# Attention outputs times w_out as three products of high and low parts, with w_out loaded raw and split on the chip

## What is computed

```python
for l in range(DEPTH):                                   # 2
    ret_o = retention(rq, rk, r_v, r_g, ret_gn_w[l])      # 256 columns
    swa_o = sliding_window_sink_attention(...)            # 384 columns
    mla_o = latent_attention(...)                         # 384 columns
    mix = jnp.concatenate([ret_o, swa_o, mla_o], axis=-1) @ w_out[l]   # 256x1024 @ 1024x1024
    x = layer_norm(DEEPNORM_ALPHA * x + mix, ln1_g[l], ln1_b[l])
    ffn = grouped_moe(x, router_w, router_bias, exp_w_gate_up[l], exp_w_down[l])
    x = layer_norm(DEEPNORM_ALPHA * x + ffn, ln2_g[l], ln2_b[l])
```

## Time and profile before

| | us |
|---|---|
| median of 3 runs | 1013.22 (1012.91 to 1014.51) |
| the profiled execution, own time | 1014.55 |
| span of its trace, first to last instruction | 1012.8 |
| TensorE busy in the span | 980.8 (97%) |
| VectorE, ScalarE, GpSimd busy | 538.0, 454.1, 92.1 |
| mean granted TensorE clock | 0.993 of full speed |

### The profile page before, as it was taken

One profiled execution on the slowest core, in us unless ns is written; L12 is line 12 of the kernel. 1 busy time (PEld: TensorE's weight loads), 2 busy tenths in 40 slices (PEclk: granted clock), 3 DMA queues, 4 the chain that ended last, 5 costly groups with the idle time before them and its releaser, 6 DMA issues.

```text
span 1012.8 us, 14203 instructions
## 1 busy us (share of the span) xinstructions
PE 980.8 (97%) x5816; PEld 809.3 (80%) x5816; DVE 538.0 (53%) x720; ACT 454.1 (45%) x643; POOL 92.1 (9%) x75
## 2 busy tenths in 40 slices
PE   8999999999999999999999999999999999999998
PEld 8997649777778789975697776787999568999997
DVE  2105637543499361264573336995568536456544
ACT  3354314522387345333452226774477434343331
POOL 0380000000000033540000000000013000000000
PEclk9999998999999999999999999999999999999999
DMA  9910403767799557031167668984223625544531
GB/s 275 292 54 1 166 1 142 284 271 295 287 361 395 135 163 201 1 105 74 42 243 273 271 253 324 375 338 167 84 83 126 218 73 199 211 170 166 202 129 42
DMA packets 88824, 189.75 MB, mean 187 GB/s; under 512 B 24864, under 2 KB 55728, under 8 KB 80448
## 3 DMA queue, kind: packets, MB, share of 16 engines
q1 hardware_dynamic: 86976, 184.23, 50.1%
q0 software_dynamic: 1504, 2.73, 1.1%
q10 hardware_dynamic: 288, 1.99, 0.5%
HBM read 187.90 MB, written 1.05 MB: 187 GB/s over the span
## 4 chain that ended last, share of the span: by engine, by line
PE 85%; ACT 5%; DVE 4%; SPq 3%; DMA 1%; issue 1%; POOL 1%; DVEq 0%; ACTq 0%
PE bank L1172 72%; PE bank L1540 2%; DVE BL L1952 2%; PE bank L1213 2%; PE bank L1570 1%; DMA WE<-in_w_in 1%; SPq L601 1%; ACT BH L855 1%; POOL QL L704 1%; PE bank L1261 1%; PE bank L1554 1%; PE bank L1243 1%; SPq L585 1%; PE bank L1247 1%; PE bank L1271 1%
## 5 line engine op out<-in xcount | busy, mean ns | idle before, releaser
L1952 DVE TENSOR_TENSOR BL<-WE,BH 128x2048 fp32r<-128x2048 f32 x72 | 163.4, 2288 | 26.0 <-ACT BH L855 25.5
L855 ACT CAST BH<-WE 128x2048 fp32r<-128x2048 f32 x72 | 136.4, 1909 | 24.5 <-PE bank L1172 24.5
L1172 PE MATMUL bank<-BH,XSB 128*128 128x512 f32 x256 | 82.3, 391 | 3.3 <-DVE BL L1952 3.3
L1172 PE MATMUL bank<-BH,XSA 128*128 128x512 f32 x256 | 81.9, 391 | 2.8 <-DVE BL L1952 2.8
L704 POOL TENSOR_TENSOR QL<-WE,QH 128x2048 fp32r<-128x2048 f32 (+2 forms) x12 | 49.3, 4126 | 345.2 <-ACT QH L847 345.2
L1172 PE MATMUL bank<-WB,XT 128*128 128x512 f32 x160 | 70.4, 596 | 3.2 <-ACT XT L922 1.3
L1172 PE MATMUL bank<-XTH,WH 128*128 128x256 f32 x256 | 72.6, 284 | 0.8 <-DVE XTL L2111 0.8
L1172 PE MATMUL bank<-XTH,WL 128*128 128x256 f32 x256 | 72.4, 283 | 0.0
L1172 PE MATMUL bank<-XTL,WH 128*128 128x256 f32 x256 | 72.4, 283 | 0.0
L969 ACT ACTIVATE XT<-bank 128x256 f32<-128x256 f32 (+1 forms) x40 | 14.5, 363 | 120.0 <-PE bank L1172 120.0
L2049 DVE SCALAR_TENSOR_TENSOR XT<-XT,small,bank 128x256 f32<-128x256 f32 (+1 forms) x40 | 18.1, 451 | 91.2 <-ACT XT L969 91.1
(11 more groups left out here) (355 smaller groups left out, 2406.8 us busy)
## 6 DMA issues: line engine op xcount, KB each, us to landing
WE<-in_exp_w_gate_up SPq DMA_DIRECT2D x64, 1024.0 KB, 9.1
WE<-in_exp_w_down SPq DMA_DIRECT2D x32, 1024.0 KB, 9.1
WE<-in_w_up SPq DMA_DIRECT2D x16, 1024.0 KB, 5.2
WE<-in_w_down SPq DMA_DIRECT2D x16, 1024.0 KB, 5.6
WE<-in_w_in SPq DMA_DIRECT2D x7, 2048.0 KB, 8.5
WE<-in_w_in SPq DMA_DIRECT2D x8, 1024.0 KB, 8.8
WB<-in_w_out SPq DMA_DIRECT2D x2, 2560.0 KB, 9.6
WE<-in_w_in SPq DMA_DIRECT2D x12, 256.0 KB, 7.3
```

The costliest lines, as they stand in the source:

```text
L855: nc.scalar.copy(BH[pair_of(b)][:, :], raw[b % N_RAW]).then_inc(blk_high[pair_of(b)], 1)
L1172: ins = nc.tensor.matmul(dst, lhsT, rhs, start=first and n == 0, stop=last and n == len(pairs) - 1)
L1952: v.tensor_tensor(BL[pair_of(b)][:, :], raw[b % N_RAW], BH[pair_of(b)][:, :].bitcast(F32), ALU.subtract).then_inc(blk_low[pair_of(b)], 1)
```

## The change

`w_out` of the first block's layers is loaded raw into the expert area `WE` in four DMAs of 1 MB, as soon as the raw projection units are used up. ScalarE casts it into `WB` (high parts) in four pieces of 128x2048, three of them ahead of its sliding-window copies and the fourth after the retention norm. GpSimd subtracts in place in `WE` (low parts). ScalarE's copies of the head outputs become casts into the high part, and VectorE subtracts them from the PSUM bank to get the low part (into `WE` behind `w_out`), which also hands the bank back: TensorE waits for VectorE now where it waited for ScalarE. Each product of `mix_part` becomes three. The second block's `w_out_2` stays as it is.

```diff
+OUT_ORDER = (1, 2, 0, 3)
...
+        out_raw = WE[:, 0:KD * D]
+        OUT_H, OUT_L = over("OUT_H", "WB", 0, [P, KD, D]), over("OUT_L", "WE", 0, [P, KD, D])
+        ATT_H, ATT_L = over("ATT_H", "XT", 0, [P, KD, SEQ]), over("ATT_L", "WE", KD * D, [P, KD, SEQ])
...
@@ SyncE
-                sp.wait_ge(ret_roped, (l + 1) * 2)
-                sp.wait_ge(*full("mla_v1", l))
-                sp.dma_start(w_out[:, 0:C_MLA, :], wo[:, 0:C_MLA, :]).then_inc(wout_in, 16)
-                sp.dma_start(w_out[:, C_MLA:KD, :], wo[:, C_MLA:KD, :]).then_inc(wout2_in, 16)
+                for u in (7, 8, 9):
+                    sp.wait_ge(unit_low[u % 3], projected(l, u))
+                for c in OUT_ORDER:
+                    sp.dma_start(out_raw.rearrange("p (c n) -> p c n", c=KD)[:, 2 * c:2 * c + 2, :], wo[:, 2 * c:2 * c + 2, :]
+                                 ).then_inc(wout_in, 16)
@@ GpSimd, behind the retention gate
+                for n, c in enumerate(OUT_ORDER):
+                    pool.wait_ge(out_high, l * 4 + n + 1)
+                    part = slice(2 * c, 2 * c + 2)
+                    nc.gpsimd.tensor_tensor(OUT_L[:, part, :], out_raw.rearrange("p (c n) -> p c n", c=KD)[:, part, :],
+                                            OUT_H[:, part, :].bitcast(F32), ALU.subtract).then_inc(out_low, 1)
@@ ScalarE, behind the copies of mla_v
+                act.wait_ge(ret_roped, (l + 1) * 2)
+                act.wait_ge(wout_in, (l + 1) * 4 * 16)
+
+                def high_out(c):
+                    part = slice(2 * c, 2 * c + 2)
+                    nc.scalar.copy(OUT_H[:, part, :], out_raw.rearrange("p (c n) -> p c n", c=KD)[:, part, :]).then_inc(out_high, 1)
+
+                for c in OUT_ORDER[:3]:
+                    high_out(c)
...
-                nc.scalar.copy(XT[:, 2:4, :], bank("swa_o0")[:, :]).then_inc(*took("swa_o0"))
+                nc.scalar.copy(ATT_H[:, 2:4, :], bank("swa_o0")[:, :]).then_inc(att_high, 1)
...
                 nc.scalar.activation(grs, grs, ACT.Exp, scale=-0.5).then_inc(gn_rooted, 1)
+                high_out(OUT_ORDER[3])
...
@@ TensorE
-                    return product(bank(f"mix{n}")[:, :], [(XT[:, k, token(n // 2)], w_out[:, k, cols]) for k in chunks], first, last)
-
-                pe.wait_ge(wout_in, (l + 1) * 16)
+                    return product(bank(f"mix{n}")[:, :], [pair for k in chunks for pair in (
+                        (ATT_H[:, k, token(n // 2)], OUT_H[:, k, cols]), (ATT_H[:, k, token(n // 2)], OUT_L[:, k, cols]),
+                        (ATT_L[:, k, token(n // 2)], OUT_H[:, k, cols]))], first, last)
+
+                pe.wait_ge(out_low, l * 4 + 2)
...
+                pe.wait_ge(out_low, l * 4 + 3)
...
-                pe.wait_ge(wout2_in, (l + 1) * 16)
+                pe.wait_ge(out_low, l * 4 + 4)
@@ VectorE, behind the maxima of latent attention
+                def low_heads(n, job, part):
+                    w = (part.stop - part.start) * SEQ
+                    dve.wait_ge(att_high, l * 5 + n)
+                    v.tensor_tensor(ATT_L[:, part, :], bank(job)[:, 0:w].rearrange("p (a b) -> p a b", b=SEQ),
+                                    ATT_H[:, part, :].bitcast(F32), ALU.subtract).then_inc(*took(job))
+
+                low_heads(1, "swa_o0", slice(2, 4))
+                low_heads(2, "swa_o1", slice(4, 5))
...
                                 ).then_inc(ret_out, 1)
+                low_heads(3, "ret_oT", slice(0, 2))
                 softmax_norm("mla", l, link, mla_p1, mla_p0)
...
+                low_heads(4, "mla_o0", slice(5, 7))
+                low_heads(5, "mla_o1", slice(7, 8))
                 for g in range(N_GRP):
```

More of the change, by code:

```diff
@@ L493, in build @@
             "rows_high", "rows_low", "gsel_ready", "sel_made", "gates_ready", "order_ready"))
+        out_high, out_low, att_high = sem("out_high"), sem("out_low"), sem("att_high")
         gathered, silu_done, hid_high, y_high = (sem(n) for n in ("gathered", "silu_done", "hid_high", "y_high"))
@@ L910, in _ @@
                 act.wait_ge(*full("swa_o0", l))
-                nc.scalar.copy(XT[:, 2:4, :], bank("swa_o0")[:, :]).then_inc(*took("swa_o0"))
+                nc.scalar.copy(ATT_H[:, 2:4, :], bank("swa_o0")[:, :]).then_inc(att_high, 1)
                 act.wait_ge(*full("swa_o1", l))
-                nc.scalar.copy(XT[:, 4, :], bank("swa_o1")[:, 0:SEQ]).then_inc(*took("swa_o1"))
+                nc.scalar.copy(ATT_H[:, 4, :], bank("swa_o1")[:, 0:SEQ]).then_inc(att_high, 1)
                 softmax_exp("mla", l, mla_p1, mla_p0, DQ ** -0.5)
@@ L920, in _ @@
                 nc.scalar.activation(grs, grs, ACT.Exp, scale=-0.5).then_inc(gn_rooted, 1)
+                high_out(OUT_ORDER[3])
                 act.wait_ge(*full("ret_oT", l))
-                nc.scalar.copy(XT[:, 0:2, :], bank("ret_oT")[:, :]).then_inc(*took("ret_oT"))
+                nc.scalar.copy(ATT_H[:, 0:2, :], bank("ret_oT")[:, :]).then_inc(att_high, 1)
                 for h in range(0, 6, 2):
@@ L926, in _ @@
                 act.wait_ge(*full("mla_o0", l))
-                nc.scalar.copy(XT[:, 5:7, :], bank("mla_o0")[:, :]).then_inc(*took("mla_o0"))
+                nc.scalar.copy(ATT_H[:, 5:7, :], bank("mla_o0")[:, :]).then_inc(att_high, 1)
                 act.wait_ge(*full("mla_o1", l))
-                nc.scalar.copy(XT[:, 7, :], bank("mla_o1")[:, 0:SEQ]).then_inc(*took("mla_o1"))
+                nc.scalar.copy(ATT_H[:, 7, :], bank("mla_o1")[:, 0:SEQ]).then_inc(att_high, 1)
                 deviations(l, 0)
@@ L1734, in _ @@
             pe.wait_ge(*read("att1", l))
-            pe.wait_ge(wout_in, (NL + 1) * 16)
+            pe.wait_ge(wout_in, (4 * NL + 1) * 16)
             for n in range(4):
@@ L1738, in _ @@
                 out_part(n, range(4), True, False)
-            pe.wait_ge(wout2_in, (NL + 2) * 16)
+            pe.wait_ge(wout2_in, 2 * 16)
             pe.wait_ge(lru_mix, 1)
```

## The result

The changed kernel took 1015.32 us (median of 20 runs), the kernel before in the same comparison 1013.43: a ratio of 1.0020, 95% interval 1.0012 to 1.0028. It is 1.2 to 2.8 us slower. The forecast was 1013.0 and a change of -0.2; the range held the time, the sign was wrong. The profiled execution of the changed kernel took 1014.43 us, its span 1012.6.

A forecast was written before the change was run, and what follows sets the result against it. TensorE, busy in 97% of the span, was taken to bound the kernel. Per layer a gain of 0.6 us less 0.5 for the clock, twice, gave -0.2: 1014.3 profiled, 1013.0 median; range 1005.2 to 1016.5.

The forecast's parts named there:

- the sign: Whole kernel: the forecast change of -0.2 us, slightly faster; chances given were faster 0.32, same 0.49, slower 0.19.
- TensorE's own work: Products with `w_out`: three fp32r products cost 0.69 us, saving 5.6 us per layer, 11.2 us in both, at most.
- The load: Raw `w_out` rows: issued at 70.4, there at about 84, wanted at 102.45; cost nothing.
- ScalarE's casts: Casts of `w_out` before the sliding-window copies and after the retention norm: 1.91 us each, hidden, three with 0.6 us to spare.
- GpSimd's pace: Low parts of `w_out`: four subtractions at 4.58 us each, from 104.4 on; the first two in time for the first part.
- The third subtraction holds up L1835: VectorE's 12-column `tensor_scalar` before the latent exponentials waits until GpSimd's subtraction ends at 118.1: 3.5 us taken, bounds 0 and 3.5.
- L1835 does not wait: Rival: VectorE's 12-column `tensor_scalar` is not held up; gain 3.6 us per layer, 7.2 in all, 1006.0 us; chance 0.25.
- What is behind it: After the 12-column `tensor_scalar`: first part starts at 119.3, 3.0 us idle; VectorE bounds the end at 150.8; layer gains 0.6.
- The clock: TensorE's granted clock may fall at its new gap: 0.5 us per layer taken, bounds 0 and 3.5.
- The term of the sum: The clock's share in the sum: +0.5 us per layer beside a gain of 0.6, times two layers.
- the rival on the other side: Rival: clock falls in the new gap, at TensorE's start at 119.3; 3.5 us per layer, +5.8 in all, 1019.0; chance 0.16.
- the bound of 1.6: Clock loss in us per layer from which that rival decides, where the sum passes +2.0 us.

The follow-up runs named there:

- experiments 1 to 3: Changed kernel with GpSimd's third subtraction after the 12-column scaling (1006.58 us), with that scaling on ScalarE (1006.73 us), or with that subtraction in halves (1008.38 us).
- experiment 1: Changed kernel with GpSimd's third subtraction held back until VectorE's 12-column scaling of the latent maxima is done: 1006.58 us, ratio 0.9931 to the kernel before.
- experiment 4: Changed kernel with identity products that add nothing to the result filling TensorE's gap before the first part: 23 took 1017.47 us, 12 took 1012.61 us.
- experiment 5: Changed kernel with TensorE's products of the heads' high parts ahead of those with their low parts: 1011.86 us, ratio 0.9979 to the kernel before.
- x1: The same run as experiment 1: 1006.58 us.
- x2: Changed kernel with 23 identity products, which add nothing to the result, ahead of TensorE's first part: 1017.47 us, ratio 1.0045 to the kernel before.
- x3: The same run as experiment 5: 1011.86 us.
- x5: Changed kernel with the 12-column scaling of the latent maxima moved from VectorE to ScalarE: 1006.73 us, ratio 0.9932 to the kernel before.
- experiment 3: Changed kernel with only GpSimd's third subtraction cut into two of 128x1024: 1008.38 us, ratio 0.9956 to the kernel before.

## Why the prediction was right and wrong

**TensorE's own work: right.** 0.69 us per three products; where the clock stayed, the first part took 8.19 to 8.41 us in the chain of waits for the forecast 8.28, and the second 5.74 for 5.52.

**The load, ScalarE's casts, GpSimd's pace: right.** The last of the four loads was issued at 71.1 and none took over 12.4 us, so the raw rows were there by 83.5 (forecast 84). Three casts in 5.50 us and the next copy not held up by them (0.94 us of slack for the forecast 0.6); three subtractions in 13.52 us, 4.5 each.

**The third subtraction holds up L1835: right.** 3.25 and 3.26 us in the two layers for the 3.5 taken. The row that the trace of before lacked is there now, and experiments 1 to 3 free the operation in three ways, each with the time that the theory gave (1006.6 for 1006.2, 1006.7 for 1006.5, 1008.4 for 1008.3). The Trainium skill, in SBUF — State Buffer, section "SBUF: two separate sides", has the lock held for a whole instruction; by that rule, the trace agrees, down to 8 columns. The rival *L1835 does not wait* did not happen, but its price was well reckoned: it gave 7.2 us, and experiment 1, which takes the wait away, brought 6.9.

**What is behind it: right.** With 0.79 us added, the first part starts at 119.06 (forecast 119.3). TensorE waits 1.40 us behind the retention transposes and VectorE has no idle time before `mix3`. The last bank is added at 152.22 for the forecast 150.8, 1.4 later: 1.63 of clock loss in the first part, less the 0.24 by which it started early.

**The clock: the step that failed.** The prediction said of it: "bounds are 0 and half of a dip of 7 us, 3.5 us per layer. I take 0.5 per layer, nearer to 0, since within the attention stretch the trace shows no dip." It fell in both layers, and cost 1.63 us in each first part of the profiled execution; filling the gap gave back 1.35 per layer over many runs. The term of the sum was mis-sized by 1.1 us per layer, 2.2 in all (0.85 and 1.7 by experiment 4): -0.2 + 2.2 is +2.0, for +1.9 measured. That these agree to 0.1 is partly luck, since the early start gives 0.5 of it back in the profiled execution, where the two layers lose 1.7.

The reason given for staying near 0 did not carry. The attention stretch had shown no dip, but it had no gap longer than 0.67 us either, and the change made one of 2.6; with that gap filled, the fall was gone. The clock was the rival on the other side. It came with half its full price, 1.63 of 3.5 us per layer, which is right at the bound of 1.6 from which it was said to decide, and it turned the sign.

## What to carry to other kernels

Before a long operation goes to GpSimd, look at what VectorE issues while it runs: a `tensor_scalar` from SBUF to SBUF waited for its end here even with 8 columns (an operation with two SBUF inputs did so in the earlier trace rows), and what matters is what hangs on that operation. Cutting GpSimd's work into pieces, placing it behind the operation, or giving the small operation to ScalarE each brought 7 to 9 us here, for a few lines of code. A gap on TensorE is to be priced with the fall of the clock behind it: here 2.1 to 2.6 us of standing still cost 1.4 to 1.6 us more. Products that add nothing to the result, no more of them than fill the gap, gave that back.

## What the hardware showed beyond that

**When the clock fell.** The changed kernel's clock fell after TensorE had started again, 1.4 us behind the gap in layer 0 (118.27 to about 119.7) and 0.3 us behind it in layer 1. In experiment 5 it fell 0.9 us after the end of the gap of 2.06 us, with four transposes done and TensorE waiting again. In experiment 1 there was a wait of 2.22 us at 30.6, far ahead of the attention end, and the clock fell within it, at 32.5. Each time it was low for 3.4 us, or for twice that behind the router of some layers. The length of a gap alone does not say whether it falls: behind waits of 1.40 us (before the second part) and of 1.64 and 1.65 us (at 48.1 and 280.5 in the changed kernel) it stayed, and behind one of 1.17 us, in layer 1 of the changed kernel, it fell at 529.3.

**The other dips, and the spread of the runs.** The dip behind the router's small products is there in every kernel, but its length moves: 6.8 us in both layers of the profiled execution of before, 3.4 in both of that of the changed kernel. In the changed kernel the one at 529 comes on top. All in all these others cost 1.7 us less there than before, as much as its two attention ends lose, so the span of its trace is no longer than before (1012.6 for 1012.8), although its median is. The dips go with the spread of the runs: over 19 runs of before on the chip of `x1`, `x2`, `x3` and `x5` the mean clock goes from 0.991 to 0.998, and the time from 1017.8 (at 0.991) to 1010.9 us (at 0.997), with 1012.6 to 1015.2 us among those at 0.995. So one profiled execution can lie 2 us to either side of the median for this reason alone, as much as the change is worth.

**Between two operations of GpSimd.** In experiment 3 VectorE got in between two subtractions. In layer 1 a `memset` follows GpSimd's fourth subtraction at once. Timeline of GpSimd, then of VectorE, in the changed kernel:

```profile
472.00 4.56 POOL L745 TENSOR_TENSOR OUT_L<-WE,OUT_H 128x2048 fp32r<-128x2048 f32 x1 [9.13 <-ACT OUT_H L923]
476.50 0.95 POOL L749 MEMSET w_bd<- 128x1024 f32 x1
```

```profile
476.08 1.45 DVE L1867 TENSOR_SCALAR WA<-WA,small 128x128 f32<-128x128 f32 x1
476.56 1.10 DVE L1868 TENSOR_SCALAR WA<-WA,small 128x256 f32<-128x256 f32 x1
```

The first `tensor_scalar` began inside the subtraction, which ended at 476.56. It ended at 477.53, behind the `memset` (477.45), where it takes 0.27 us alone. So VectorE did not get its turn between the two, and a `memset`, which reads nothing, holds it up as well. Of the eight profiled kernels in which a `tensor_scalar` waited there, seven show this (in experiment 1 it took 3.03 us, across both); in `x5` it got in between and ended at 469.40, with the subtraction (469.31). Nothing waited for it in any of them. Cutting GpSimd's work into pieces worked where it was tried, with two subtractions; these rows say that it need not work for every pair, and what decides it is open.
